# Expert value rows gathered by token, one block later, and summed in four strips of the array

## The reference

```python
def block(args):                      # attention, one block of 128 queries
    s = jnp.einsum('bqhd,bkhd->bhqk', qn, k_nope) + jnp.einsum('bqhr,bkr->bhqk', qr, k_rope)
    s = jnp.where(k_pos[None, :] <= q_pos[:, None], s, MASK_VALUE)
    p = jax.nn.softmax(s, axis=-1).astype(v.dtype)
    ...
def block(xt):                        # PEER, one block of 128 tokens
    q = (xt @ w_q).reshape(PEER_BLOCK, PEER_HEADS, 2, PEER_QDIM // 2)
    s = jnp.einsum('thpd,hpkd->thpk', q, sub_keys).astype(F32)
    s_top, i_top = lax.top_k(s, K)
    ...
    ids = jnp.take_along_axis(cand_i, pos, axis=-1)
    gate = jax.nn.softmax(best_s, axis=-1).astype(xt.dtype)
    u = jnp.take(u_tab, ids, axis=0)
    act = jax.nn.gelu(jnp.einsum('td,thkd->thk', xt, u))
    vv = jnp.take(v_tab, ids, axis=0)
    return jnp.einsum('thk,thkd->td', gate * act, vv)
```

## Time and profile before

| | us |
|---|---|
| median of 3 timed runs | 4198.71 (4193.22 to 4201.24) |
| span of the profiled execution | 4468.8 |
| PE busy | 3063.4 |
| DVE busy | 2584.9 |
| POOL busy | 2296.7 |
| ACT busy | 599.9 |

### The profile page before, as it was taken

How to read it: one execution, slowest core, us unless ns; L and a number is a source line. 1 busy time by engine, 2 the same in 40 slices (tenths; PEclk the granted TensorE clock), 3 DMA queues, 4 the chain that set the end, 5 groups by cost and what they waited for, 6 DMA issues and landing times.

```text
span 4468.8 us, 39267 instructions
## 1 busy us (share of the span) xinstructions
PE 3063.4 (69%) x8713; PEld 1506.8 (34%) x8713; DVE 2584.9 (58%) x7140; ACT 599.9 (13%) x1572; POOL 2296.7 (51%) x2229
## 2 busy tenths in 40 slices
PE   4737775768757686586856777666776868756666
PEld 2413342324423243233432334233442424422222
DVE  4376547655475565756556655666547655565443
ACT  1101111021101111011111121112110111100010
POOL 1025546565454554555545554556445555556665
PEclk8669898988979888798988988888887988878888
DMA  2238787787878878777877878778687777878887
GB/s 111 66 117 302 264 296 266 272 315 249 284 252 318 300 271 290 268 270 280 298 267 262 298 269 293 261 271 307 251 271 282 285 280 279 282 266 312 316 307 268
DMA packets 404508, 1197.16 MB, mean 268 GB/s; under 512 B 53202, under 2 KB 123908, under 8 KB 404356
## 3 DMA queue, kind: packets, MB, share of 16 engines
q0 software_dynamic: 294912, 1073.87, 66.4%
q1 hardware_dynamic: 109444, 121.41, 8.4%
HBM read 1189.37 MB, written 5.77 MB: 267 GB/s over the span
## 4 chain that ended last, share of the span: by engine, by line
PE 28%; DVE 27%; issue 16%; DMA 13%; POOL 6%; another core or an unknown queue 5%; DVEq 4%; ACT 1%; POOLq 1%; ACTq 0%; SPq 0%
PE vsum L1060 16%; DMA v_rows<-in_peer_v,ids 10%; DVE u_rows L486 10%; POOL u_rows L397 4%; PE bank L1079 3%; DVE scr L751 3%; DMA ring<-in_peer_w_q 3%; PE bank L1213 2%; POOL v_rows L402 2%; DVE scr L748 2%; PE bank L1201 1%; PE bank L1093 1%; DVE scr L753 1%; DVE scr L700 1%
## 5 line engine op out<-in xcount | busy, mean ns | idle before, releaser
L1060 PE MATMUL vsum<-v_rows,diag 128*128 128x512 f32 x4096 | 2145.0, 678 | 887.1 <-DMA v_rows<-in_peer_v,ids 538.9
L402 POOL DMA_INDIRECT v_rows<-in_peer_v,ids x1024 | 1142.2, 1115 | 1382.8 <-PE vsum L1060 998.6
L1060 PEld LDWEIGHTS vsum<-v_rows,diag 128*128 128x128 f32 x4096 | 861.7, 218 | 2131.4 <-issue 1390.9
L486 DVE CUSTOM_DVE_ANT_0 u_rows<-u_rows,xn_cur 128x1024 f32<-128x1024 f32 x1024 | 1204.0, 1223 | 424.8 <-DMA u_rows<-in_peer_u,ids 372.7
L397 POOL DMA_INDIRECT u_rows<-in_peer_u,ids x1024 | 1095.1, 1069 | 435.4 <-issue 283.4
L935 ACT ACTIVATE diag<-ident,hid_w 128x128 f32<-128x128 f32 x1024 | 320.2, 389 | 470.0 <-PE vsum L1060 288.5
L929 ACT ACTIVATE hid_e<-hid_e 128x8 f32<-128x8 f32 x128 | 26.8, 209 | 2073.7 <-DVE hid_e L496 2049.2
L392 POOL COPY ids<-ids_ring 128x8 uint32 (+1 forms) x128 | 40.3, 315 | 331.3 <-DVE ids_ring L806 330.7
L1213 PE MATMUL bank<-nT,ring 128*128 128x128 f32 x1024 | 145.8, 310 | 88.7 <-DMA ring<-in_peer_w_q 76.0
L1046 PE MATMUL bank<-ident,scr 128*128 128x128 f32 (+1 forms) x488 | 80.8, 307 | 170.6 <-DVE scr L517 82.4
L1079 PE MATMUL bank<-win,nT 128*128 128x512 f32 (+1 forms) x384 | 164.7, 584 | 21.2 <-issue 19.9
(11 more groups left out here) (216 smaller groups left out, 2310.9 us busy)
## 6 DMA issues: line engine op xcount, KB each, us to landing
ring<-in_w_out SPq DMA_DIRECT2D x64, 512.0 KB
ring<-in_peer_w_q SPq DMA_DIRECT2D x64, 512.0 KB
u_rows<-in_peer_u,ids POOLq DMA_INDIRECT x1024
v_rows<-in_peer_v,ids POOLq DMA_INDIRECT x1024
win<-in_w_in SPq DMA_DIRECT2D x2, 7808.0 KB, 26.5
ring<-in_mla_w_uq SPq DMA_DIRECT2D x16, 384.0 KB
ring<-in_mla_w_ukv SPq DMA_DIRECT2D x8, 512.0 KB
qT<-in_norm_ffn SPq DMA_DIRECT2D x8, 512.0 KB
```

The lines of the kernel that those rows point to most:

```text
L402: pool.indirect_dma_start(v_rows[:, j % VR, :], None, v_tab, bass.IndirectOffsetOnAxis(ids[:, q, j:j + 1], 0)).then_inc(v_in[j % VR], 16)
L486: v.tensor_tensor_reduce(out=u_rows[:, j, :], in0=u_rows[:, j, :], in1=xn_cur[:], scale=1.0, scalar=0.0, op0=ALU.mult, op1=ALU.add, accum_ ...
L1060: ins = mm(vsum[:, n * 512:(n + 1) * 512], diag[:, j, :], v_rows[:, j % VR, n * 512:(n + 1) * 512], start=False, stop=False, skip_group_ch ...
```

## The change

1. **Gathers of v go by token.** A new transposed table of ids, `idsT`, lets one gather fetch for one token the rows of its 128 slots, a slot in each partition. The size is the same, 512 KB, and there are as many gathers. The weighted sum of a token is then a product of one weight column (128 slots) with 128 x 1024 rows.
2. **One block later.** The v rows of step s-2 are gathered and summed in the front of step s, beside the dot products of step s-1. POOL alternates one v gather and one u gather. The last step's v rows come after everything else.
3. **Four strips.** PE takes four tokens at a time, one for each 32-column strip of the array: the stationary operand is 128 x 32 with the weight column at place m and zeros beside it (a window into `wx`, which ACT fills by `spread`, one small copy for four tokens), the output is 32 partitions of `vsum`. The records are as many as before: 16 for four tokens.
4. **One gelu for a block.** `hidden` makes the gelu of all 128 slots at once: three DVE operations and two ACT operations (square, tanh) on 128 columns, then a transposition on PE.
5. **Buffers.** `u_rows` goes from 8 to 5 slots (`UR`), `v_rows` from 4 to 8 (`VR`), freed by fours.
6. **Places.** 32 units of four slots are spread over 19 places by the table `TURNS` (two units in most of the early ones, one each around attention and routing, three each in the two weight streams, four at the end).
7. **Unrolled.** No hardware loop is left; block and layer numbers are constants. Attention works on (b+1) x 128 keys in block b. The residual is added to the sum of experts by DVE (`summed`), through two more transfers by SP for each step, and no longer through an identity matmul.

```diff
-GR = 8
-NG = SLOTS // GR
-TURN = 4
-VR = 4
-V_START = VR + 1
+UR = 5
+VR = 8
+VG = 4
+NVG = SLOTS // VG
+WR = 4
+
+TURNS = [2, 2, 2, 1, 2, 2, 1, 2, 1, 1, 1, 1, 3, 3, 1, 1, 1, 1, 4]
...
+            def gather_u(s, k):
+                n = SLOTS * s + k
+                if n >= UR:
+                    pool.wait_ge(u_free, n - UR + 1)
+                pool.indirect_dma_start(u_rows[:, n % UR, :], None, u_tab,
+                                        bass.IndirectOffsetOnAxis(ids[:, s % 2, k:k + 1], 0)).then_inc(u_in[n % UR], 16)
+
+            def gather_v(s, k):
+                n = SLOTS * s + k
+                if n >= VR and k % VG == 0:
+                    pool.wait_ge(v_free, n // VG - VR // VG + 1)
+                t = token(k // VG, k % VG)
+                pool.indirect_dma_start(v_rows[:, n % VR, :], None, v_tab,
+                                        bass.IndirectOffsetOnAxis(idsT[:, s % 2, t:t + 1], 0)).then_inc(v_in[n % VR], 16)
+
+            for p in range(STEPS + 1):
+                if p > 0:
+                    pool.wait_ge(idsT_ready, p)
+                for k in range(SLOTS):
+                    if p > 0:
+                        gather_v(p - 1, k)
+                    if p < STEPS:
+                        if k == 0:
+                            pool.wait_ge(ids_ready, p + 1)
+                        gather_u(p, k)
...
+            def hidden(s, fresh):
+
+                v.scalar_tensor_tensor(hid_g[:], hid[:], 0.5, gates_cur[:], ALU.mult, ALU.mult).then_inc(hid_ready, 1)
+                if fresh:
+                    v.tensor_copy(xn_cur[:], feat[:])
+                dve.wait_ge(sq_ready, s + 1)
+                v.scalar_tensor_tensor(hid_a[:], hid_a[:], 1.0 / GELU_A, hid[:], ALU.add, ALU.mult).then_inc(arg_ready, 1)
+                if fresh:
+                    v.tensor_copy(gates_cur[:], gates_next[:])
+                dve.wait_ge(th_ready, s + 1)
+                v.scalar_tensor_tensor(hid_g[:], hid_a[:], 1.0, hid_g[:], ALU.add, ALU.mult).then_inc(w_ready, 1)
...
+            def spread(s, m0, n):
+
+                for m in range(m0, m0 + n):
+                    g = NVG * s + m
+                    if g >= WR:
+                        act.wait_ge(v_free, g - WR + 1)
+                    a_.activation(wx[:, g % WR, :, 32:33], wT[:].rearrange("p (c m) -> p c m", c=VG)[:, :, m:m + 1],
+                                  ACT.Copy).then_inc(wx_ready, 1)
...
-            def experts(g, half):
-
-                pe.wait_ge(diag_ready, 2 * g + half + 2)
-                for j in range(VR * half, VR * half + VR):
-                    pe.wait_ge(v_in[j % VR], 16 * (2 * g + half + 1))
+            def sums(s, m0, n):
+
+                for m in range(m0, m0 + n):
+                    g = NVG * s + m
+                    if m == 0 and s > 0:
+                        pe.wait_ge(x_new, s)
+                    pe.wait_ge(wx_ready, g + 1)
+                    for c in range(VG):
+                        r = VG * g + c
+                        pe.wait_ge(v_in[r % VR], 16 * (r // VR + 1))
                     for n in range(2):
-                        ins = mm(vsum[:, n * 512:(n + 1) * 512], diag[:, j, :], v_rows[:, j % VR, n * 512:(n + 1) * 512],
-                                 start=False, stop=False, skip_group_check=True)
+                        for c in range(VG):
+                            ins = mm(vsum[32 * c:32 * c + 32, n * 512:(n + 1) * 512], wx[:, g % WR, c, 32 - m:64 - m],
+                                     v_rows[:, (VG * g + c) % VR, n * 512:(n + 1) * 512],
+                                     start=m == 0, stop=m == NVG - 1, skip_group_check=True)
                     ins.then_inc(v_free, 1)
```

613 lines of the change are left out of this document (278 added, 335 removed).

## The result

| us | before | after |
|---|---|---|
| timed median | 4195.97 (4189.85 to 4201.24, 4 runs) | 3998.21 (3982.89 to 4016.06, 4 runs) |
| span of the profiled execution | 4468.8 | 3995.8 |

The ratio is 0.953 (95% interval 0.949 to 0.956): 198 us faster, where I forecast 506 faster (3690 us; the time lies in the range of 3440 to 4040). The profiled execution of the kernel after took 3997.5 us, like its timed runs. My sum in "the profile's time" was 3930; the profile has 3995.8. So the sum missed by 1.7%, and the factor of 0.94, by which I brought it to timed runs, missed by 6%. One run of the kernel "four last" (experiment 8), 4029 us at a granted clock of 0.56 for 0.67, was in a slower state and is left out of what follows.

The account below looks back on a forecast made before the run. PE's sums and the gathers of v were taken to wait for each other, with four slots of v. 280 + 375 + 6 x 445 + 605 = 3930 us, x 0.9396 = 3690 us (3550 to 3830; wider range 3440 to 4040).

Parts of the forecast that it names:

- the scaling: Whole kernel: the sum of 3930 us in the profile's time times 0.9396 gives 3690 us timed.
- Routing: Routing stretch of a full step: DVE sets it, four routes of 21.6 us plus 18 of dots, 105 us.
- nothing stalls: Rival: routes at step 0's speed (84 us), DMA full elsewhere, 407 us a step; timed 3415 us, chance 0.12.
- Weight streams: Stretch with 24 slots: DMA sets it, 66 us of pairs plus 25 of weights, 91 us.
- Up to the scores: Front of a step: 47 us end of step, then 156 us to the first scores by POOL and DVE.
- Attention: Attention stretch with 16 slots: DVE 42 us at full key range, less for shorter keys, 46 us.
- Tail: Behind step 7's routing: pairs 385 us, 128 gathers of v alone 175, about 15 of last work; 605 us.
- Strips: PE's sums: a record overlaps only its neighbour's, factor two, 3.4 us a unit, all hidden while the clock is high.
- Clock: Rival: PE's clock at 1.2 GHz in most stretches, front matmuls double, 25 us a step; timed 3850 us, chance 0.12.
- Gathers never full: Rival: gathers move only 321 GB/s, 3.26 us a pair, 489 us a step; timed 4008 us, chance 0.13.
- Serial strips at a high clock: Rival: strips run one after the other on PE, 490 us a step; sum 4287, timed 4028 us, chance 0.07.
- Instruction prefetch: Within the rival nothing stalls: if branches breaking prefetch made the idle pieces, unrolling takes them all.

Follow-up runs that it names:

- four last: The kernel of experiment 8 with four dot products of the last route moved behind the write of the next ids; 3903 us.
- experiment 8: The kernel after with half of each route's dot products inside it and the end-of-step units spread over the routes; 3900.1 us, ratio 0.930.
- second profile: The kernel before, unchanged, profiled again; 4195.4 us timed, span 4199.8.
- experiment 7: The kernel after with every gather of u and v fetching 2 KB of each row for 4 KB; 3837.2 us, ratio 0.916.
- experiment 5: The kernel after with each unit's records ordered strip by strip, both halves of one strip, then the next; 4015.1 us.
- experiment 4: The kernel after with every strip product of v issued twice; 4145.5 us, 147 more than after.
- experiment 6: The kernel after with all groups but a block's first written to one strip; 4388.6 us where before takes 4479, ratio 0.980.
- experiment 2: The kernel before with every hardware loop written out as a plain one, nothing else; 4102.4 us, ratio 0.979.
- experiment 9: The kernel of experiment 8 with seven slots of u for five and six of v for eight; 4277.2 us, ratio 1.021.

## Why the prediction was right and wrong

**The step that failed is the scaling.** "The timed median is 0.94 of the span, so 3930 x 0.9396 = 3690 us" took the excess of the profiled execution for a common factor. It was 269 us, nearly all idle time (4468.8 less 4199.8), of the kernel before, about the amount by which it is slower in one of the five series (4479, 281 more than 4198). That the profile on record was made on such a chip is read from its time and its 85 idle pieces of over 1 us (81 and 79 there, 5 and fewer elsewhere), not known. The steps carry the excess: 531.7 us there, 492.1 in the second profile. My sum, built of durations and of the waits that I gave to after, held little of it (the idle pieces of the routes), and must not be scaled. Of the miss of 308 us, 240 are this factor and 66 the sum. The other side of the same error is the saving: I set the new step of 445 beside 526.8, and the one that was timed is 492 (461 for step 1).

**In the sum the terms missed on both sides and nearly cancelled, which was luck.** The sum's 1.7% is not a sign of how well its parts were known.
- *Routing, 105, measured 77.5.* I carried the idle pieces of the earlier trace rows over (21.6 us a route, where the dots are taken off). After has 20.4 us a route with four dots, 15.8 without, step 0's speed, as two starts of a route's first maximum show:

```profile
2417.85 0.86 DVE L720 MAX8 scr<-scr 128x8 f32<-128x128 f32 x4
...
2438.21 0.87 DVE L720 MAX8 scr<-scr 128x8 f32<-128x128 f32 x4
```

  Here "nothing stalls" was nearer (84), though gathers ran beside the routes, which I had held against it.
- *Weight streams, 91, measured 119.* I gave each stretch as many pairs as it has dots. Over steps 2 to 7 the routing has 27.5 gathers, attention 22.8, and the weight streams 62.5: 31 pairs for my 24. What the full slots of u hold back in the routing is caught up where DVE waits. These seven pairs are 19 us at my 2.73; the rest is a rate of 352 GB/s for my 384.
- *Up to the scores, 203 with the end of step, measured 228.* The end was right (48.7 for 47). Then POOL issued 111 gathers for my 102, at 1.42 us each, and stood some 17 us for slots of u and 9 for slots of v: 179 us for 156.
- *Attention, 46, measured 36;* step 0, 280 for 264; step 1, 375 for 358.
- *Tail, 605 for 611.* The sum is right by luck. The pairs took 368 us for my 415, since the earlier trace rows's 1.99 us is the longest issue and not the usual one beside dot products (1.20 us in the mean, 1.00 in the median, in after). v alone took 222 us for my 175, since eight slots of v do not keep DMA full (experiment 7). That 128 gathers of v stand alone behind the last pairs was right. (My sign of "some 560 us" there did not fit my own sum of 605.)

**Strips.** The price was 3.4 us a unit by a factor of two; it is 1.92 us at the full clock and 3.64 at the low one, 100 us a step. "A record can overlap only its neighbour's" is wrong: experiment 5 has four in a row on one strip and its units are 1.94 us. By the Trainium skill (TensorE: Matmul & The Clock Gate, "Part 3: Packing small matmuls") three strips give 2.38 times; four gave 3.7 here. Cover was not complete either: experiment 4 gives 0.31 us of time for each us of PE's sums.

**Rivals.** *Clock:* it fell to 0.67 in the mean, 0.54 in the routing, as the rival said. What it costs no run isolates. The sum without this rival's 25 us a step fell short by 66 us in all, and DVE's waits for PE's banks fell from 505 us (before, unrolled) to 167, while its waits for rows of u rose from 404 to 897; so I read it that matmuls at the low clock are mostly covered by waits for rows, but that is argued. *Gathers never full* has nearly the same time (4008), but its mechanism holds in parts only: the pairs of the tail moved 408 GB/s, v alone 305, less even than its 321. *Serial strips at a high clock* was 4287 before the scaling, and experiment 6 spans 4408.7 on the slower chip. *Instruction prefetch:* the Trainium skill (Runtime: NRT & Kernel Launch, "Instruction fetch mechanics") says that a branch breaks it. I let the row of step 0 outweigh that; experiment 2 shows that loops cost 14 us in every step, 96 to 101 us in all. How much of it is prefetch is open. The second profile of before agrees with the rule where the outer loop turns: DVE stands five times for 3.2 to 3.9 us, and packets of an instruction queue move about 2 us before it goes on; that is 17 of its 144 us. The other 127 us are 426 pieces under 1 us at many lines inside the loops, a quarter of their time before one small operation ("issue 31.1" below), and what they are no run tells:

```profile
L504 DVE TENSOR_TENSOR hid_w<-hid_e,hid 128x8 f32<-128x8 f32 x128 | 21.5, 168 | 32.2 <-issue 31.1
```

**Where the gain comes from.** In the one series that has all four kernels (4198.2, 4097.0, 4067.9, 4007.1) it is 101 us by the loops, 29 by the short keys and 61 by everything else. By the cuts the rest is 8 us in step 0, 83 in step 1 (no v rows yet) and 17 in each of the other six, 193 in all, less 129 in the tail. So one block later costs about 46 us by itself, 129 at the end less the 83 in step 1, whose v rows it moves there (read from the cuts, not from a run that changes it alone). It is paid for by the 17 us in each full step and the 8 in step 0. These come from v by token, the strips, one gelu, the buffers and the order of the gathers together, which were not taken apart. That the deeper buffer of v is needed for it is seen in experiment 9, where two slots fewer (and two more of u) cost 377 us. The kernel before with more slots of v was not run.

## What to carry to other kernels

When a profiled span and the timed runs differ by several per cent, look for the rows in which the difference lies before scaling anything by it, and take a second profile: idle pieces without a releaser may belong to that execution or that program form, and a rewritten kernel may not have them. Count the work that a queue does in a stretch by what its buffers let it do there, not by what the stretch consumes. When a sum comes out right, look whether its parts did: two halves of the tail missed by 47 us each, one up and one down. Before a deep restructuring, write out the hardware loops alone: here that was half of the whole gain.

## What the runs showed of the hardware

- The kernel before takes 4189 to 4198 us in four series and 4479 in a fifth; the rate in the same window of another kernel was 409 and 367 GB/s. How much a kernel suffers depends on its form: 6.7, 4.1 and 1.8%. What the idle pieces are made of stays open. On the slower chip they are there in the unrolled form too (242 us on DVE's timeline with short keys, for 17), and of the 85 in the profile on record 10 lie within 1 us of a packet of an instruction queue. In after's form they are not in the routes.
- An issue of a gather takes POOL 0.94 us where DVE does nothing, with rows of 4 KB, and 0.95 with rows of 2 KB. Beside dot products it takes 1.20 and 1.32 in the mean, and up to 2.00. The Trainium skill (SBUF — State Buffer, "Who interferes with whom") says that a DVE instruction with two inputs in SBUF contends with a GpSimd instruction that reads SBUF. The trace agrees in so far as the dot products have two such inputs and lengthen the issue; that the shared port is the cause, no run shows.
- Products of 32 columns on four strips overlap 3.7 times, also when each strip's four records are issued in a row.
